# One root per norm, applied to matmul outputs in PSUM, in a two-block model kernel

## The reference, cut to what matters

```python
def rms_norm(x, g):
    xf = x.astype(jnp.float32)
    y = xf * lax.rsqrt(jnp.mean(xf * xf, axis=-1, keepdims=True) + RMS_EPS)
    return (y * g.astype(jnp.float32)).astype(x.dtype)

def conv_glu_ffn(h, w_up, conv_w, w_down):
    up = causal_dwconv(h @ w_up, conv_w)          # 3 taps along positions
    gate, val = jnp.split(up, 2, axis=-1)
    return (jax.nn.silu(gate) * val) @ w_down
...
        h = rms_norm(x, ffn_norm_g[l])
        x = x + conv_glu_ffn(h, w_up[l], ffn_conv_w[l], w_down[l])
    return rms_norm(x, final_norm_g)
```

## Time and profile before

| | |
|---|---|
| median of 3 runs | 2775.7 us (2772.16 to 2789.74) |
| profiled execution | 2774.72 us, of which the span from first to last instruction is 2772.9 us |
| TensorE busy | 2569.5 us, 93% of the span; mean granted clock 0.961 |
| DVE, ACT, POOL busy | 954.4, 624.0 and 766.4 us (34%, 23%, 28%) |
| chain that ended last | TensorE 84%, DVE 8%, ACT 3%, POOL 2% |

### The profile page before, as it was taken

The page is one execution under the profiler, slowest core; times in us unless marked ns, Lnnn a source line. Parts: engine busy times, 40 slices in busy tenths (PEclk is TensorE's granted clock), DMA queues, the critical chain, the costliest instruction groups (busy, mean ns, idle before and its releaser), DMA issues.

```text
span 2772.9 us, 35958 instructions
## 1 busy us (share of the span) xinstructions
PE 2569.5 (93%) x15625; PEld 2000.1 (72%) x15625; DVE 954.4 (34%) x1199; ACT 624.0 (23%) x897; POOL 766.4 (28%) x500
## 2 busy tenths in 40 slices
PE   5999999999999799899999999997699999768998
PEld 3778777777778577578888888884477866545676
DVE  3112123231474541233333333333230126545521
ACT  3100122222231210221111111112232125424420
POOL 3222333332331274123233232331122210201121
PEclk8989999999999899899999999998899999979999
DMA  2311222222200263111111111110311112000014
GB/s 92 114 39 38 86 82 76 76 76 76 61 10 4 79 224 93 46 39 47 51 45 52 47 45 53 45 46 15 99 46 38 46 54 43 1 8 1 1 40 127
DMA packets 194121, 156.88 MB, mean 57 GB/s; under 512 B 15674, under 2 KB 175649, under 8 KB 193738
## 3 DMA queue, kind: packets, MB, share of 16 engines
q1 hardware_dynamic: 193994, 155.00, 18.5%
HBM read 125.58 MB, written 29.40 MB: 56 GB/s over the span
## 4 chain that ended last, share of the span: by engine, by line
PE 84%; DVE 8%; ACT 3%; POOL 2%; issue 1%; SPq 1%; DMA 0%; POOLq 0%; DVEq 0%; ACTq 0%
PE gp L851 17%; PE gp L853 17%; PE gp L852 17%; PE sm L853 4%; PE sm L852 4%; PE sm L851 4%; PE sm L873 2%; PE sm L1445 2%; PE gp L1349 2%; PE gp L1365 2%; POOL merged L781 1%; PE sm L1382 1%; DVE h_tmp L1840 1%; DVE att_s L2279 1%; DVE h_lo L1850 1%
## 5 line engine op out<-in xcount | busy, mean ns | idle before, releaser
L851 PE MATMUL gp<-h_hi,w_hi 128*128 128x512 f32 x1632 | 658.4, 403 | 44.6 <-DVE h_lo L1850 43.3
L853 PE MATMUL gp<-h_hi,w_lo 128*128 128x512 f32 x1632 | 641.9, 393 | 0.0
L852 PE MATMUL gp<-h_lo,w_hi 128*128 128x512 f32 x1632 | 641.5, 393 | 0.0
L720 POOL CAST w_hi<-w_raw 128x1024 fp32r<-128x1024 f32 (+1 forms) x165 | 174.4, 1057 | 1406.3 <-PE gp L853 1025.4
L722 POOL TENSOR_TENSOR w_lo<-w_raw,w_hi 128x1024 fp32r<-128x1024 f32 x173 | 429.7, 2484 | 107.2 <-ACT w_hi L1683 85.2
L851 PEld LDWEIGHTS gp<-h_hi,w_hi 128*128 128x128 f32 x1632 | 309.7, 190 | 138.9 <-DVE h_lo L1850 41.4
L852 PEld LDWEIGHTS gp<-h_lo,w_hi 128*128 128x128 f32 x1632 | 310.8, 190 | 65.6 <-issue 4.1
L853 PEld LDWEIGHTS gp<-h_hi,w_lo 128*128 128x128 f32 x1632 | 309.9, 190 | 66.5
L1934 DVE TENSOR_TENSOR_SCAN sb_run<-sb_keep,ones_row 128x128 f32<-128x128 f32 (+7 forms) x32 | 77.1, 2450 | 318.2 <-POOL sb_keep L730 318.2
L851 PE MATMUL sm<-h_hi,w_hi 128*128 128x512 f32 x352 | 136.9, 389 | 0.0
L852 PE MATMUL sm<-h_lo,w_hi 128*128 128x512 f32 x352 | 136.9, 389 | 0.0
(11 more groups left out here) (408 smaller groups left out, 3955.1 us busy)
## 6 DMA issues: line engine op xcount, KB each, us to landing
w_raw<-in_w_in SPq DMA_DIRECT2D x79, 512.0 KB, 4.3
w_raw<-in_w_up SPq DMA_DIRECT2D x44, 512.0 KB, 3.8
gates_spill<-gate_out SPq DMA_DIRECT2D x32, 512.0 KB, 3.1
gate_in<-gates_spill SPq DMA_DIRECT2D x32, 512.0 KB, 4.3
w_raw<-in_w_down SPq DMA_DIRECT2D x22, 512.0 KB, 3.3
x_back<-x_spill SPq DMA_DIRECT2D x16, 512.0 KB, 4.0
x_tok<-in_x SPq DMA_DIRECT2D x8, 512.0 KB, 7.3
x_spill<-x_t SPq DMA_DIRECT2D x1, 4096.0 KB, 12.4
```

Of the source, the lines that this page charges most:

```text
L720: pool.tensor_copy(w_hi[:, t % 2, 0:n], w_raw[:, t % 2, 0:n]).then_inc(s["w_high"], 1)
L851: pe.matmul(o, wh, hi[:, k0 + k, c], start=(k == 0), stop=False)
L852: pe.matmul(o, wh, lo[:, low[k] if low else k0 + k, c], start=False, stop=False)
L853: mm = pe.matmul(o, wl, hi[:, k0 + k, c], start=False, stop=(k == n - 1))
```

## The change

The norms ahead of the feed-forward part and of the second block's input products are taken apart. The products no longer take the normed tile: their input is x times the norm's gain alone, and the root is multiplied into the outputs in PSUM. Part by part:

- As soon as DVE has added tile d of `x_mid`, ACT writes `h_hi` from `x_mid` times the gain (`x_high`), DVE writes `h_lo` in one instruction (`x_low`), and ACT squares the tile (`x_squared`). This happens between the outputs of `w_o`, and between those of the last two down blocks.
- POOL adds squares 0 to 6 up (`accumulate`, 6 additions per norm); TensorE sums that total and square 7 with ones: 4 matmuls per norm (`x_sums`) in place of 16; ACT makes the root in place of them (`x_rooted`).
- The first product behind a norm (`follow`) goes tile by tile over both halves and waits for `h_split` before each tile; `x_sums` stands behind it in TensorE's order.
- Each of the 44 up outputs is multiplied in place in PSUM by the root on DVE before ACT's first tap; the 24 input outputs are taken out of PSUM by DVE with that multiplication, the last 8 in place, with ACT's Silu behind.
- Final and second norm are joined: h = x·g_fin·g_2, and one root stands for both: 1/sqrt(mean(x²(g_fin² + eps)) + eps²). `fin_gain` and `fin_weight` are 128x8 columns made once at the start. The final norm's own root (`x_sums(2)`, behind input product 5) and its 8 multiplications (L1840 before) move on DVE to input products 6 to 9, and the store of `x_mid` (L607) behind weight load 12 of that stage.
- The last two down blocks go over the two g tiles with the tile outermost: the parts of the first g tile for 4 outputs, then those of the second, each with a wait for its own g tile.
- DVE's work on the second block's positions and head norms is interleaved with the taking of outputs. `x_back`, `nrt` and a few scratch tiles get other places.

```diff
--- before.py
+++ after.py
...
+        def x_square(e, k):
+            if e == 0:
+                return (cos_t if k % 2 else mid_sq)[:, :]
+            return end_sq[:, k % 4, :]
+        def x_total(e):
+            return (sum_0, sum_1, sum_2)[e][:, :]
+        def x_scale(e):
+            return (up_scale, in_scale, fin_scale)[e][:, :]
...
-            sp.wait_ge(s["h_ready"], 3 * KT)
-            sp.dma_start(x_spill, x_mid[:, :, :]).then_inc(s["x_out"], 16)
...
+                if t == T_IN2 + 12:
+                    sp.wait_ge(s["x_normed"], KT)
+                    sp.dma_start(x_spill, x_mid[:, :, :]).then_inc(s["x_out"], 16)
...
+            def accumulate(e, k):
+                pool.wait_ge(s["square"], KT * (e + 1) + k + 1)
+                if k == 1:
+                    pool.wait_ge(s["square_used"], KT + e)
+                else:
+                    pool.wait_ge(s["x_acc"], 6 * e + k - 1)
+                pool.tensor_tensor(x_total(e), x_square(e, 0) if k == 1 else x_total(e), x_square(e, k), ALU.add) \
+                    .then_inc(s["x_acc"], 1)
+            for d in range(KT):
+                split_weights(T_WO + 2 + d)
+                if 1 <= d < KT - 1:
+                    accumulate(0, d)
+            for t in range(T_FFN + 2, T_IN2 + 1):
+                split_weights(t)
+            for k in range(1, 4):
+                accumulate(1, k)
+            split_weights(T_IN2 + 1)
+            pool.wait_ge(s["h_split"], 3 * KT)
+            for k in range(4, 7):
+                accumulate(1, k)
+            for n in range(4):
+                split_weights(T_IN2 + 2 + n)
+                for k in ((1,), (2,), (3, 4), (5, 6))[n]:
+                    accumulate(2, k)
...
+            def follow(t, p):
+                pe.wait_ge(s["w_split"], t + 1)
+                for z in range(2):
+                    pe.wait_ge(s[f"p_free{z}"], slot_frees(p + z))
+                for k in range(KT):
+                    wait("h_split")
+                    wh, wl = ring(t, P * k, P * k + P)
+                    for half in range(2):
+                        c = slice(HALF * half, HALF * half + HALF)
+                        o = slot(p)[:, c]
+                        pe.matmul(o, wh, h_hi[:, k, c], start=(k == 0), stop=False)
+                        pe.matmul(o, wh, h_lo[:, k, c], start=False, stop=False)
+                        mm = pe.matmul(o, wl, h_hi[:, k, c], start=False, stop=(k == KT - 1))
+                mm.then_inc(s["p_ready"], 1)
+            def x_sums(e):
+                pe.wait_ge(s["x_acc"], 6 * e + 6)
+                pe.wait_ge(s["square"], KT * (e + 2))
+                for half in range(2):
+                    c = slice(HALF * half, HALF * half + HALF)
+                    pe.matmul(sm[:, 2 + half, :], ones[:, :], x_total(e)[:, c], start=True, stop=False)
+                    mm = pe.matmul(sm[:, 2 + half, :], ones[:, :], x_square(e, KT - 1)[:, c], start=False, stop=True)
+                mm.then_inc(s["square_used"], 1)
...
-            norm(1)
-            for n in range(4):
-                whole(T_FFN + n, P_FFN + n, h_hi, h_lo, "h_split" if n == 0 else None)
+            follow(T_FFN, P_FFN)
+            x_sums(0)
+            for n in range(1, 4):
+                if n == 3:
+                    pe.wait_ge(s["root"], 2)
+                whole(T_FFN + n, P_FFN + n, h_hi, h_lo)
...
-            pe.wait_ge(s["g_split"], FT)
             for u in range(2):
-                down(FT // 2 - 1, u, 4 * u)
-            norm(2)
-            norm(3)
-            wait("h_split", KT)
+                t = T_IN2 - 2 + u
+                pe.wait_ge(s["w_split"], t + 1)
+                for k in range(2):
+                    pe.wait_ge(s["g_split"], FT - 1 + k)
+                    for j in range(4):
+                        p = P_IN2 - 8 + 4 * u + j
+                        if k == 0:
+                            pe.wait_ge(s[f"p_free{p % 2}"], slot_frees(p))
+                        wh, wl = ring(t, HALF * k + P * j, HALF * k + P * j + P)
+                        for half in range(2):
+                            c = slice(HALF * half, HALF * half + HALF)
+                            o = slot(p)[:, c]
+                            pe.matmul(o, wh, g_hi[:, k, c], start=(k == 0), stop=False)
+                            pe.matmul(o, wh, g_lo[:, k, c], start=False, stop=False)
+                            mm = pe.matmul(o, wl, g_hi[:, k, c], start=False, stop=(k == 1))
+                        if k == 1:
+                            mm.then_inc(s["p_ready"], 1)
...
-                whole(T_IN2 + n, P_IN2 + n, h_hi, h_lo)
+                if n == 0:
+                    follow(T_IN2, P_IN2)
+                    x_sums(1)
+                else:
+                    whole(T_IN2 + n, P_IN2 + n, h_hi, h_lo)
+                if n == 5:
+                    x_sums(2)
...
+            def x_high(k, gain):
+                act.activation(h_hi[:, k, :], x_mid[:, k, :], ACT.Copy, scale=gain).then_inc(s["high"], 1)
+            def x_squared(e, k):
+                ring = 2 if e == 0 else 4
+                if k >= ring:
+                    act.wait_ge(s["x_acc"], 6 * e + max(1, k - ring))
+                act.activation(x_square(e, k), x_mid[:, k, :], ACT.Square,
+                               scale=fin_weight[:, k:k + 1] if e == 1 else 1.0).then_inc(s["square"], 1)
+            def x_rooted(e):
+                act.wait_ge(s["square_used"], KT + e + 1)
+                wait.after(act.activation(x_scale(e), sm[:, 2:4, :].rearrange("p a b -> p (a b)"), ACT.Ln,
+                                          bias=RMS_EPS ** 2 if e == 1 else RMS_EPS, scale=1.0 / D))
+                act.activation(x_scale(e), x_scale(e), ACT.Exp, scale=-0.5).then_inc(s["root"], 1)
...
-            for z in range(2):
-                act.wait_ge(s[f"p_free{z}"], frees_before(P_FFN))
-            norm(1, x_mid)
-            split_h()
+            logs_and_exps()
+            for d in range(KT):
+                p = P_WO + d
+                act.wait_ge(s[f"p_free{p % 2}"], frees_before(p) + 1)
+                x_high(d, pcol("ffn_g", d))
+                x_squared(0, d)
+            x_rooted(0)
...
-                act.wait_ge(s["p_ready"], 12 * i + (p + 1))
+                act.wait_ge(s["scaled"], 4 * i + (5 + buf))
...
-            for z in range(2):
-                act.wait_ge(s[f"p_free{z}"], frees_before(P_IN2))
-            norm(2, x_mid)
-            norm(3, x_mid, "x_normed")
-            split_h()
+            logs_and_exps()
+            for d in range(KT):
+                p = P_IN2 - KT + d
+                act.wait_ge(s[f"p_free{p % 2}"], frees_before(p) + 1)
+                x_high(d, fin_gain[:, d:d + 1])
+                x_squared(1, d)
+            x_rooted(1)
+            for k in range(2):
+                x_squared(2, k)
...
+            def x_low(k, gain):
+                wait("high")
+                dve.scalar_tensor_tensor(h_lo[:, k, :], x_mid[:, k, :], gain, h_hi[:, k, :].bitcast(F32),
+                                         ALU.mult, ALU.subtract).then_inc(s["h_split"], 1)
...
-            norm(x_mid, "ffn_g")
+                x_low(d, pcol("ffn_g", d))
...
+                ps = slot(p)
+                dve.wait_ge(s["p_ready"], 12 * i + (p + 1))
+                dve.tensor_tensor(ps, ps, up_scale[:, :], ALU.mult).then_inc(s["scaled"], 1)
...
-            norm(x_mid, "fin_g", x_mid)
-            norm(x_mid, "g2")
+            add_down(FT // 2 - 1, 0, p0, True)
+            add_down(FT // 2 - 1, 1, p0 + 4, True)
+            x_low(KT - 1, fin_gain[:, KT - 1:KT])
...
+            dve.wait_ge(s["root"], 3)
+            for n in range(24):
+                p = P_IN2 + n
+                dve.wait_ge(s["p_ready"], p + 1)
+                ps = gp[:, p % 2, :]
+                if n < 16:
+                    dst = in_tile(n)[:, ::-1] if 4 <= n < 8 else in_tile(n)
+                    dve.tensor_tensor(dst, ps, in_scale[:, :], ALU.mult).then_inc(s[f"p_free{p % 2}"], 1)
+                else:
+                    dve.tensor_tensor(ps, ps, in_scale[:, :], ALU.mult).then_inc(s["scaled"], 1)
+                if 2 <= n < 13:
+                    n2_normed(n - 1)
...
```

154 lines of the change are left out of this document (94 added, 60 removed).

## The result

The changed kernel took 2685.12 us (median of 4 runs, 2680.07 to 2707.38) beside 2782.72 us for the kernel before (4 runs, 2772.16 to 2790.57). The ratio is 0.9667, with a 95% interval of 0.96 to 0.9734: 3.3% faster. The prediction was 2686 us. The profiled execution took 2684.0 us, with a span of 2681.3 us (2772.9 before). TensorE's busy time fell from 2569.5 to 2519.4 us; its mean granted clock rose from 0.961 to 0.971.

What follows compares the result with a forecast made beforehand. TensorE bounds the long stages (685.00 of 685 us busy); two norm stretches of 50.7 and 107.8 us leave it waiting. 35.0 + 58.3 - 4.8 = 88.5 us off 2774.72 gives 2686 us, range 2677 to 2703.

Steps and rivals of the forecast that it cites:

- First place: Norm ahead of the feed-forward part: last addition to end of x_sums takes 15.7 us in place of 50.7, 35.0 us gained.
- Loop: Inside the feed-forward part: 44 multiplications in PSUM on DVE cost 0, with up to 1.9 us more of latency.
- The 1.9 us of cover: Feed-forward turns: way from up product to g tile becomes about 9.0 us, beside another up product of 10.88 us.
- Rival (d): Feed-forward part: multiplication in place in PSUM far dearer; at 12 us each, 2783 us, slower than before; chance 2%.
- Second place: End of feed-forward part through joined norm and first input product with x_sums: 49.5 us in place of 107.8, 58.3 us gained.
- The clock loss of 1.7 us: Last down blocks: behind two gaps of 1.3 and 2.3 us TensorE runs at half clock, about 1.7 us of work lost.
- The collision: End of feed-forward part: `x_low` on DVE waits for POOL's splits and additions, moving the last addition by +2.7 us.
- Rival (c): Root gates TensorE because x_sums waits for POOL's last addition: +12 us, 2698 us, inside the range; chance 5%.
- (a): Clock stays at half through both down quarters and the following product: +23.8 us, 2710 us; chance 4%.
- (b): DVE becomes the bound of the input products, 2.5 us each for products 3 to 11: +22 us, 2708 us; chance 5%.
- Input products and attention: Second block's input products and attention start: x_sums(2) adds 3.5 us, the last output's way 1.3; together 4.8 us lost.

## Why the prediction was right

**First place: right.** Predicted 15.7 us, measured 16.1; gained 34.6 for 35.0 predicted. The run with this half alone gained 35.0 in all, 34.8 of it up to the end of the loop. The gap of 1.52 us (1.3 to 1.4 predicted) kept the clock at 1.00. The run with one slot's wait shows that this gap can be removed.

**Loop: right.** Multiplications of 1.23 us, TensorE at 100%. The 1.9 us of cover were of the right size but somewhat too large; the rows give 1.4. 1.22 us more cost nothing, three multiplications more opened a gap. Rival (d) asked for a much dearer multiplication in place; 1.233 us is its mean over 22.

**Second place: right in its sum, by terms that cancelled.** 49.5 us predicted and measured. The two short gaps were 1.35 and 2.03 us (1.3 and 2.3 predicted). The clock loss of 1.7 us behind them did not come in the first profile (clock 1.00) but did in the second one of the same kernel (0.58 from 1849 to 1853), where the first input matmul came 28.3 us behind the first stop in place of 26.7. Behind the gap of 6.39 us the first input product took 13.8 us in place of 10.9, a loss of 2.9 us in place of 1.7. The collision was too small in the sum: +2.7 for splits and additions, while the additions alone cost 2.75. So what the missing clock loss gave back, the larger loss behind the long gap and DVE's longer chain took. That the stretch came out at 49.5 us to the tenth is luck; in the second profile of the same kernel it was 50.2. The rule of the Trainium skill ("SBUF — State Buffer", "Who interferes with whom") agrees with the trace here: `h_lo`, with two SBUF operands, went from 1.28 to 2.3 us and more beside POOL, while the 44 multiplications with one PSUM and one SBUF operand all took 1.231 to 1.233 us, with POOL busy for 213.58 of 685.40 us.

**Rival (c): not met, but near.** x_sums didn't wait for POOL: POOL was done 2.0 us earlier, 1.1 in the second profile. As soon as the product started earlier, POOL's sum became the releaser, with 5.80 us.

**Rivals (a) and (b): not met.** The matmuls took 0.39 us again from 1875.15 on, 6 us behind the gap. (The prediction's reason against (a) was read too short: behind the gap of 7.84 us in the kernel before, the clock rose again only 5.8 us later, at 1891.2, and not within 5.) And DVE's 80.12 us in 280 us of input products put no gap over 0.5 us on TensorE.

**Input products and attention: a term too small.** x_sums(2) cost the 3.5 us predicted and the later start 1.3 (gap 2.58 for 1.32). What the step left out is that this longer gap stands ahead of sparse matmuls and a second gap of 2.46 us, and that the clock then stayed at half, for 2.6 us more. So 7.4 us were lost where 4.8 were forecast. Moving the wait gave 510.1, 511.3 and 512.1 us for the tail in three kernels; in seven profiles with the gap of 2.58 us, two of them of the change, it was 513.2 to 514.6, against 510.4 to 510.9 with the gap of 1.32. The gap itself is 1.3 of that; the rest was 1.2 to 2.6 us.

**The time itself.** 2684.0 us against 2686.2 predicted for the profiled execution is closer than the steps deserve. The change's own stages gave 85.5 us where 88.5 were forecast. The 6.1 us upstream are luck, since they lie in code that the change leaves alone; 0.9 us went the other way, by which the time exceeds the span more than before.

## What to carry to other kernels

A factor that is the same for all channels of a position need not stand ahead of a matmul over channels: apply it to the output, and squares, sums and root run beside the product. Then look at what takes its place, engine by engine: here the chain through DVE and POOL over the last tile, where moving TensorE's waits only moved the idle time. Before adding work to an engine that has room on average, count the latency between the output and its use; one multiplication of 1.2 us was free here, and three cost 3.1 us per turn.

## What the runs showed of the hardware

**The same code ran at either clock for some 50 us on end.** Ahead of the output projection, one window of the kernel after and one of the change with its attention wait moved, both in the mixer's stage of 64x64 matmuls, which no edit touches:

```profile
900.00:910.00 10.00, 9.25 (x285) 8.71 (x280) 2.13 (x12) 0.00 (x0) 0.00 (x0) 1.00 0.02 6
```

```profile
900.00:910.00 10.00, 9.55 (x172) 9.07 (x170) 1.42 (x8) 0.00 (x0) 0.00 (x0) 0.50 0.01 3
```

In the first TensorE ran at 2.4 GHz, in the second at 1.2 GHz from 893 to 941 us, with 172 matmuls done in place of 285 in the window. Everything behind it comes some 16 to 24 us later. Two of the fourteen profiled executions show this (marks at 1072 and 1074, the others 1050 to 1056), and timed runs of 2702 to 2707 us beside others near 2685 fit it, though only the profiled ones can be looked into.

**Gaps of the same length, different clocks.** Behind gaps of 1.35 and 2.03 us the change ran at 1.00 in one execution and at 0.58 in another. Of the seven profiled executions with these two gaps, in kernels with the same code there, five show the half clock behind them and two don't. A window of the second execution of the change:

```profile
1849.00:1853.00 4.00, 4.00 (x13) 3.10 (x11) 1.84 (x2) 1.92 (x2) 0.00 (x0) 0.58 0.00 0
```

Behind the gap of 2.58 us at the attention's start, the eight matmuls took 3.06 to 3.78 us in six profiles and 1.99, the time at full clock, in the seventh. At the attention's start, gaps of 1.31 and 2.46 us left the clock at 1.00 for 12 us in one kernel and at 0.86 on average in another with the same code there. So a single profile says of such a gap what happened once. What decides between the two wasn't found.
